# Seven half products for twelve of the 22 up tiles of each SwiGLU block, in a two-layer fp32 transformer on one Trainium2 core

## The reference

```
def rms_norm(x, g):
    y = xf * lax.rsqrt(jnp.mean(xf * xf, axis=-1, keepdims=True) + NORM_EPS)
    return (y * g.astype(jnp.float32)).astype(x.dtype)
def swiglu(h, w1, w3, w2):
    return (jax.nn.silu(h @ w1) * (h @ w3)) @ w2
...
        x = x + 0.5 * rms_norm(swiglu(rms_norm(x, g[0]), ffn_w1[l, 0], ffn_w3[l, 0], ffn_w2[l, 0]), g[1])
...
        x = x + 0.5 * rms_norm(swiglu(rms_norm(x, g[4]), ffn_w1[l, 1], ffn_w3[l, 1], ffn_w2[l, 1]), g[5])
```

## Time and profile before

| what | value |
|---|---|
| three runs | 1973.55, 1974.46, 1974.59 us; median 1974.46 us |
| profiled execution: device time | 1972.13 us |
| its span | 1970.0 us |
| mean granted TensorE clock | 0.993 of full speed |

### The profile page before, as it was taken

One profiled execution on the slowest core, in us unless ns is written; L12 is line 12 of the kernel. 1 busy time (PEld: TensorE's weight loads), 2 busy tenths in 40 slices (PEclk: granted clock), 3 DMA queues, 4 the chain that ended last, 5 costly groups with the idle time before them and its releaser, 6 DMA issues.

```text
span 1970.0 us, 25894 instructions
## 1 busy us (share of the span) xinstructions
PE 1926.0 (98%) x9965; PEld 1652.0 (84%) x9965; DVE 976.3 (50%) x1438; ACT 699.4 (36%) x1099; POOL 48.6 (2%) x55
## 2 busy tenths in 40 slices
PE   8999999999999999999999999999988999999998
PEld 7888888978889888888988888889877898888888
DVE  5444432476757544432385444324766485444323
ACT  5232222355536232322352323223554453232222
POOL 0000000011100000000000000000000000000000
PEclk9999999999999999999999999999999999999999
DMA  5333333322212333333233332333211223333331
GB/s 162 107 98 94 100 93 106 87 65 76 75 54 87 106 90 101 94 101 96 84 86 107 85 106 85 96 104 83 60 42 45 65 78 95 106 87 102 102 94 43
DMA packets 347366, 174.65 MB, mean 89 GB/s; under 512 B 18478, under 2 KB 346268, under 8 KB 347292
## 3 DMA queue, kind: packets, MB, share of 16 engines
q1 hardware_dynamic: 346528, 172.51, 30.8%
q10 hardware_dynamic: 764, 1.11, 0.2%
HBM read 171.50 MB, written 2.10 MB: 88 GB/s over the span
## 4 chain that ended last, share of the span: by engine, by line
PE 89%; DVE 8%; ACT 1%; issue 1%; POOL 0%; DMA 0%; SPq 0%; DVEq 0%; ACTq 0%
PE acc L1425 26%; PE acc L1426 26%; PE acc L1427 26%; PE sco L1425 3%; PE sco L1427 2%; PE sco L1426 2%; DVE sqs L1035 1%; DVE y L982 1%; DVE xT L989 1%; DVE xg L959 1%; DVE wl L924 1%; DVE mx L1123 1%; PE acc L1610 1%; PE aux L1453 1%; PE aux L1425 1%
## 5 line engine op out<-in xcount | busy, mean ns | idle before, releaser
L1425 PE MATMUL acc<-xg,wh 128*128 128x512 f32 (+1 forms) x1816 | 673.1, 371 | 6.5 <-DVE wl L924 2.9
L1426 PE MATMUL acc<-xg,wh 128*128 128x512 f32 (+1 forms) x1816 | 667.3, 367 | 0.0
L1427 PE MATMUL acc<-xg,wl 128*128 128x512 f32 (+1 forms) x1816 | 667.2, 367 | 0.0
L924 DVE TENSOR_TENSOR wl<-raw,wh 128x1024 fp32r<-128x1024 f32 (+1 forms) x332 | 385.6, 1187 | 156.8 <-ACT wh L560 151.7
L1425 PEld LDWEIGHTS acc<-xg,wh 128*128 128x128 f32 x1816 | 343.6, 189 | 64.7 <-DVE wl L924 3.2
L1426 PEld LDWEIGHTS acc<-xg,wh 128*128 128x128 f32 x1816 | 343.5, 189 | 57.0 <-issue 1.4
L1427 PEld LDWEIGHTS acc<-xg,wl 128*128 128x128 f32 x1816 | 343.5, 189 | 55.8
L560 ACT ACTIVATE wh<-raw 128x1024 fp32r<-128x1024 f32 (+1 forms) x332 | 327.1, 1023 | 130.4 <-PE acc L1427 85.9
L1427 PE MATMUL acc<-hT,wl 128*128 128x512 f32 (+1 forms) x704 | 255.2, 362 | 0.0
L1426 PE MATMUL acc<-hT,wh 128*128 128x512 f32 (+1 forms) x704 | 255.2, 362 | 0.0
L1425 PE MATMUL acc<-hT,wh 128*128 128x512 f32 (+1 forms) x704 | 255.2, 362 | 0.0
(11 more groups left out here) (242 smaller groups left out, 1854.6 us busy)
## 6 DMA issues: line engine op xcount, KB each, us to landing
raw<-in_ffn_w_dram SPq DMA_DIRECT2D x240, 512.0 KB, 4.6
raw<-in_ffn_w_dram SPq DMA_DIRECT2D x32, 384.0 KB, 3.4
raw<-in_moba_w_qkv_dram SPq DMA_DIRECT2D x24, 512.0 KB, 3.8
raw<-in_moba_w_o_dram SPq DMA_DIRECT2D x8, 512.0 KB, 3.9
raw<-in_mla_w_o_dram SPq DMA_DIRECT2D x8, 512.0 KB, 4.0
xin<-in_x_dram SPq DMA_DIRECT2D x4, 512.0 KB, 5.6
raw<-in_mla_w_dq_dram SPq DMA_DIRECT2D x4, 512.0 KB, 4.1
raw<-in_mla_w_uq_dram SPq DMA_DIRECT2D x8, 256.0 KB, 2.8
```

Of the source, the lines that this page charges most:

```text
L924: v.tensor_tensor(wl[:, slot, 0:tiles], raw[:, slot, 0:tiles], f32(wh[:, slot, 0:tiles]), ALU.subtract).then_inc(w_lo, 1)
L1425: t.matmul(dst, w_h, m_h, start=start, stop=False)
L1426: t.matmul(dst, w_h, m_l, start=False, stop=False)
L1427: return t.matmul(dst, w_l, m_h, start=False, stop=stop)
```

## The change

Six of the 22 up tiles (`FS`) stay as they were. The other sixteen come in four turns of four (`TURN`): three fast tiles and a plain one.

A fast tile takes w1 and w3 of one inner tile together with the two halves of K (`KH` = 4 of the eight K tiles) and the two token halves as 2x2 blocks, and computes them with seven products in Winograd's form of Strassen's method in place of eight: 7 x 4 x 3 = 84 matmuls of 256 columns, where there were 48 of 512. Four products take sums of weight blocks (`ssum`, and one half of the raw w3 tile rewritten in place) and four take sums of x blocks (`tsum`, split into `tx`, once for each FFN). The products land in `sums`, `pairs` and `rest` (two banks joined), and are added up by one ACT copy (`m1_copied`) and four DVE additions (`second_sum`, `rows`). A fast tile has units of 8, 8 and 12 tiles, which fill three and a half of the four slots, and each fast or plain tile of a turn begins at slot 0; before, units went round the four slots.

So that the products can be added without `Rb`, x is multiplied by gain and norm factor once (`xn`: `x_full` on ACT, two DVE multiplications), and its parts take the place of those of the unnormed x in `xg` (`x_part`) while PE passes from tile 5 to tile 6.

The inner tiles are kept in fp32 (`hid`) through the up half; their high and low parts are made in seven groups (`HID`) where the down half begins. Of a turn's raw tiles each is loaded when the first two weight splits of the tile two before it are done. At the start of the down half ACT makes the high parts of groups 0 and 1, tile 21's silu, the split of the first down unit, groups 2 and 3, the split of the second unit, and then groups and splits in turn. Stages outside the FFNs keep their instructions.

The diff is cut to: the units; ACT's turn (`next_hi` is the weight copy to fp32r); DVE's multiplication by `Rb`, weight sums, product sums, turn (`tile_lo` is the low part of weights) and start of the down half; PE's turn. In the third FFN `x_full` waits for the last key/value unit.

```diff
+    FS, TURN, KH = 6, 4, KD // 2
+    FAST_U = [(UT, 1), (UT, 1), (UT + KH, 0)]
+    TURN_U = FAST_U * (TURN - 1) + [(UT, 1)] * 2
+    TURNS, GT = (KF - FS) // TURN, TURN - 1
+    FFN_U = [(UT, 1)] * (2 * FS) + TURN_U * TURNS + [(n, 1) for n in DOWN] * KD
...
+                        if c < TURN - 1:
+                            g = G0 + GT * it + c
+                            act.wait_ge(prod_psum, 2 * g + 1)
+                            s.activation(usum[:, 0], tile_banks(c)[0][:, half(0)], COPY).then_inc(m1_copied, 1)
+                            next_hi(c, w, 0)
+                            next_hi(c, w, 1)
+                            if c < TURN - 2:
+                                next_hi(c, w, 2)
+                            if q == 0 and c == 1:
+                                x_part(4)
+                            act.wait_ge(rows_ready, 2 * g + 1)
+                            gate(f, T[0][:])
+                        elif not last:
+                            next_hi(c, w, 0)
+                            act.wait_ge(unit_done, w + 1)
+                            gate(f, tile_banks(c)[0][:])
+                            next_hi(c, w, 1)
+                            next_hi(c, w, 2)
...
+                for k in range(0, KD, KH):
+                    dve.wait_ge(xf_ready, KD * nth + k + KH)
+                    v.tensor_tensor(xn[:, k:k + KH], xn[:, k:k + KH],
+                                    Rb[:].unsqueeze(1).broadcast_to([P, KH, S]), ALU.mult).then_inc(xn_ready, 1)
+                plain(2)
+                if kv is not None:
+                    between()
...
+                def outer_sums(w, g, slot, counts):
+                    for a in range(2):
+                        dve.wait_ge(raw_full[slot + a], counts[a])
+                    dve.wait_ge(w_lo, w)
+                    v.tensor_tensor(ssum[:, UT:UT + KH], raw[:, slot, 0:KH], raw[:, slot + 1, 0:KH], ALU.subtract
+                                    ).then_inc(ssum_ready, 1)
+                    dve.wait_ge(ssum_ready, 4 * g + 1)
+                    v.tensor_tensor(raw[:, slot + 1, 0:KH], raw[:, slot + 1, 0:KH], raw[:, slot + 1, KH:KD], ALU.add
+                                    ).then_inc(ssum_ready, 1)
+                def inner_sums(g, slot):
+                    dve.wait_ge(ssum_ready, 4 * g + 2)
+                    v.tensor_tensor(ssum[:, 0:KH], raw[:, slot + 1, 0:KH], raw[:, slot, 0:KH], ALU.subtract
+                                    ).then_inc(ssum_ready, 1)
+                    dve.wait_ge(ssum_ready, 4 * g + 3)
+                    v.tensor_tensor(ssum[:, KH:UT], raw[:, slot, KH:KD], ssum[:, 0:KH], ALU.subtract
+                                    ).then_inc(ssum_ready, 1)
...
+                def second_sum(g, banks):
+                    dve.wait_ge(m1_copied, g + 1)
+                    dve.wait_ge(prod_psum, 2 * g + 2)
+                    v.tensor_tensor(usum[:, 3], banks[0][:, half(1)], usum[:, 0], ALU.add).then_inc(usum_ready, 1)
+                def rows(f, w, g, banks):
+                    rest = banks[2][:, 0:3 * HALF].rearrange("p (a s) -> p a s", a=3)
+                    dve.wait_ge(unit_done, w + 3)
+                    dve.wait_ge(usum_ready, 2 * g + 1)
+                    dve.wait_ge(rows_ready, 2 * g)
+                    v.tensor_tensor(usum[:, 1:3], rest[:, 1:3], usum[:, 3:4].broadcast_to([P, 2, HALF]), ALU.add
+                                    ).then_inc(usum_ready, 1)
+                    dve.wait_ge(usum_ready, 2 * g + 2)
+                    v.tensor_tensor(T[0][:], banks[1][:], usum[:, 0:2].rearrange("p a s -> p (a s)"), ALU.add
+                                    ).then_inc(rows_ready, 1)
+                    dve.wait_ge(hid_ready, F0 + f)
+                    v.tensor_tensor(T[2][:].rearrange("p (a s) -> p a s", a=2), rest[:, 0:2],
+                                    usum[:, 2:3].broadcast_to([P, 2, HALF]), ALU.add).then_inc(rows_ready, 1)
...
+                        if c < TURN - 1:
+                            g = G0 + GT * it + c
+                            if n < TURN - 1:
+                                outer_sums(w_next, g_next, slot, counts)
+                            tile_lo(w_next, 0, slot)
+                            second_sum(g, banks)
+                            if n < TURN - 1:
+                                inner_sums(g_next, slot)
+                            tile_lo(w_next, 1, slot)
+                            rows(f, w, g, banks)
+                            if n < TURN - 1:
+                                tile_lo(w_next, 2, slot)
+                            dve.wait_ge(rows_ready, 2 * g + 2)
+                            gated(f, dst, T[2][:])
+                            if q == 0 and c == 1:
+                                x_part(4)
+                        elif not last:
+                            outer_sums(w_next, g_next, slot, counts)
+                            inner_sums(g_next, slot)
+                            tile_lo(w_next, 0, slot)
+                            dve.wait_ge(unit_done, w + 2)
+                            gated(f, dst, banks[1][:])
+                            tile_lo(w_next, 1, slot)
+                            tile_lo(w_next, 2, slot)
...
+                d0 = down_unit(u)
+                hidden_lo(0)
+                hidden_lo(1)
+                split(d0)
+                dve.wait_ge(unit_done, d0)
+                gated(KF - 1, hid[:, KF - 1], tile_banks(KF - 1)[1][:])
+                hidden_lo(2)
+                hidden_lo(3)
+                split(d0 + 1)
+                hidden_lo(4)
+                split(d0 + 2)
...
+                        pe.wait_ge(hid_ready, KF * nth + f - 1)
+                        pe.wait_ge(w_lo, w + 1)
+                        if c == TURN - 1:
+                            first(xb_lo, 5 * nth + 5)
+                            tiles(sums[:], 0, 0, UT, from_x(xg)).then_inc(unit_done, 1)
+                            pe.wait_ge(w_lo, w + 2)
+                            tiles(pairs[:], 1, 0, UT, from_x(xg)).then_inc(unit_done, 1)
+                            continue
+                        first(xb_lo, 5 * nth + 1)
+                        tiles(sums[:, half(0)], 0, 0, KH, quarter(0, 0)).then_inc(prod_psum, 1)
+                        first(xb_lo, 5 * nth + 3)
+                        tiles(pairs[:, half(0)], 0, KH, KH, quarter(1, 0)).then_inc(unit_done, 1)
+                        pe.wait_ge(w_lo, w + 2)
+                        first(tx_lo, 4 * nth + 2)
+                        tiles(rest[:, HALF:2 * HALF], 1, 0, KH, xsum(0))
+                        tiles(rest[:, 0:HALF], 1, KH, KH, xsum(1)).then_inc(unit_done, 1)
+                        pe.wait_ge(w_lo, w + 3)
+                        first(tx_lo, 4 * nth + 4)
+                        pe.wait_ge(m1_copied, GT * TURNS * nth + GT * it + c + 1)
+                        tiles(sums[:, half(1)], 2, 0, KH, xsum(2)).then_inc(prod_psum, 1)
+                        first(xb_lo, 5 * nth + 4)
+                        tiles(pairs[:, half(1)], 2, KH, KH, quarter(1, 1))
+                        tiles(rest[:, 2 * HALF:3 * HALF], 3, 0, KH, xsum(3)).then_inc(unit_done, 1)
```

More of the change, by code:

```diff
@@ L1535, in ffn @@
                         unit(u + 4 + a, acc[a][:], from_x(xg))
[L1536 to L1541 removed]
+                for i in range(4 * first, 2 * FS - 1):
+                    pe.wait_ge(evacuated, r + i - 3)
+                    unit(u + i, acc[i % 4][:], from_x(xg))
```

386 lines of the change are left out of this document (297 added, 89 removed).

## The result

| | before | after |
|---|---|---|
| median of the runs | 1974.01 us (4 runs, 1973.01 to 1974.59) | 1946.62 us (4 runs, 1943.06 to 1947.78) |
| profiled execution | 1972.13 us, span 1970.0 | 1946.04 us, span 1943.8 |
| ratio | | 0.9859, 95% interval 0.9842 to 0.9876 |

The account below looks back on a forecast made before the run. PE's matmul stream was taken as the bound: 1972.1 - 38.4 (products) + 0.7 (normed x) + 4.0 (down half) + 4.7 (third FFN) + 1.6 (clock) = 1944.7, plus 2.3 for the median: 1947 us; own range 1942 to 1952, 0.8 range 1937 to 1960.

Parts of the forecast that it names:

- PE's pace: Up tiles: a 256-column matmul takes 0.120 us, so a fast tile takes 10.08 us against a plain tile's 10.88.
- The 38.4 us: Products in the up halves: 0.80 us less per fast tile, 48 fast tiles, certain if PE is never kept waiting.
- DVE in a fast tile: DVE's twelve operations take about 9.6 of 10.08 us: nearly saturated, but no PE wait inside the turns.
- With all of DVE's operations 10% longer: Sensitivity in the turns: PE would wait 3.4 us an FFN; at 15% 7.5, at 20% 11.6.
- the rival at 1960: DVE operations 10% slower than the rows say, adding 13.6 us of PE waits; chance 0.18.
- DVE the bound: Rival: DVE 20% slower bounds the fast tiles, 46 us of waits, 1993 us, slower than before; chance 0.05.
- Going over to the normed x: At tile 6 PE's second product waits 0.2 us for the third quarter part, four times: 0.7 us.
- Start of the down half: PE waits 1.0 us for the second unit's low part, behind DVE's groups 2 and 3; four times, 4.0 us.
- The third FFN: Tile 3: PE waits 4.4 us for `ckv_diag` behind DVE's two multiplications of x; 4.7 us with tile 3's first-unit delay.
- the 0.3: Third FFN: `x_full` on ACT delays the split of tile 3's first unit, making PE wait 0.3 us.
- The clock: After the third FFN's 4.4 us pause, one half-clock stretch costs 1.6 us, bounds 0 and 1.6.
- The sum: All terms give 1944.7 us for the profiled execution; 2.3 more for the median of the runs gives 1947.

Follow-up runs that it names:

- the halved loop: Kernel before the change with every matmul of the looped up tiles cut into two of 256 columns: 2023.08 us against 1971.71, ratio 1.0264.
- two extra additions: Changed kernel with two more DVE additions of 512 elements in each fast tile, results unused: 1950.82 us, ratio 0.9886.
- the missing product: Changed kernel with one of a fast tile's seven products (12 of 84 matmuls) left out, output wrong: 1905.02 us, ratio 0.9648.
- the key/value move: Changed kernel with the third FFN's DVE multiplications of x put behind `ckv_diag` and tile 4's weight splits: 1944.23 us, ratio 0.9867.
- both moves: Changed kernel with x's multiplications behind `ckv_diag` in the third FFN, and `hidden_lo(2)` ahead of DVE's wait for the last up product: 1941.02 us, ratio 0.9841.
- turns of eight and of sixteen: Both moves plus 14 fast tiles per FFN in two turns of eight, or 15 in one of sixteen: 1932.81 us (0.9807) and 1931.42 us (0.9794).
- the pause of 2.1: Both moves with 15 fast tiles, and ACT making the first three parts of the normed x ahead of tile 5's silu: 1926.15 us, ratio 0.9765.

## Why the prediction was right, point by point

**PE's pace.** 0.120 a matmul, 10.08 a fast tile, 0.80 to 0.82 less: right, to the hundredth, and confirmed alone by the halved loop. The 38.4 us that were priced came. By the formula of the Trainium skill's page "TensorE: Matmul & The Clock Gate", section "Back-to-back issue gap", the isolated gap for 256 columns is 109.2 ns, and by this estimate the products would have saved 57 us. The trace does not agree: the measured 120 is 10% above it, in the kernel before, the changed kernel and the halved loop alike.

**DVE in a fast tile.** 9.6 us was the sum, 9.45 the measure: right that it is the nearly full engine and that no wait arises inside the turns. Wrong was the sensitivity beside it. "With all of DVE's operations 10% longer" was given 3.4 us an FFN and 15% 7.5; two extra additions lengthen DVE's fast tile by 13%, from 9.45 to 10.65, and cost 0.53. (Two more operations in a queue are not the same as slower ones all along it, which no run has.) Two links of the chain can be read: its fast tile was 0.15 too long, and it left 0.4 us to spare at the third units of the first turn, where the rows have 1.57 and 1.88; in the later turns it had 1.4 and the rows have 1.7 to 1.9. So the rival at 1960 was priced too high for its condition, while "DVE the bound" had its mechanism and place right, as the missing product shows.

**Going over to the normed x.** 0.2 an FFN; the starts give 0.17 on one interval (0.29) and 0.10 on the next (0.22): 0.27.

**Start of the down half.** Mechanism, place and releaser right, 1.0 predicted, 1.18 measured: the pause is 1.04, and the restart's 0.1 was not in the term.

**The third FFN.** 4.7 predicted, 4.05 measured (of -5.23 against -9.29). Tile 3's first unit was not delayed by `x_full`: it starts at 1024.70, 0.81 behind the mean of squares, as in the kernel before, so the 0.3 was nothing, and DVE made the way to the diagonal in 0.2 to 0.3 less. What the prediction did not see is that the wait is a backlog of DVE and not only the order of the two multiplications. Its chain of times does carry `x_full`'s 5.1 us, since DVE's first split ends at 1040.2 there, but as the reason it names only the 4.5 us of the order, and only that was moved. DVE's late start of 4.1 us is about as large, and which part of the 3.8 us it is stays open.

**The clock.** The step that failed as stated: one stretch of 1.6 was put down as sure to follow. In the first profile it did not come. In six profiled executions with this pause at the spread it came in five. It cost 1.6 us in three of them (1.59, 1.64, 1.59) and 2.4 and 2.6 in two, where the spread's own matmuls ran at half clock too, above the bound of 1.6 that was given. With a pause of the same length at tile 6 it came in all four (the key/value move, both moves, turns of eight and of sixteen), and after the pause of 2.1 it did not come.

**The sum.** Without the clock the terms give -29.0, the trace -28.4. The profiled execution then stands 2.2 higher in code that did not change: 1.1 before tile 2 of the first FFN (42.46 against 41.36), where eleven more matmuls of 256 columns start 0.21 apart in place of 0.12, and 1.0 in the attention of layer 1, with six half-clock stretches against five (below). The forecast was 1944.7 for the profiled execution, which took 1946.04, and added 2.3 for the median, which lies only 0.6 above it. That the median falls within 0.4 us of the forecast is partly chance: a missing 1.6 and an unforeseen 2.2 in the trace, and an allowance 1.7 too large on top of it.

## What to carry to other kernels

Fewer columns in smaller matmuls are worth what the fixed part of each matmul leaves: price both forms from starts in the trace first (here 0.2267 and 0.120, so an eighth fewer columns are 7% of the tile). When another engine fills up, compare its work with the bound engine's per tile, and add up what it overdraws over the full tiles that follow each other; set that against the spare time at the first place where the bound engine wants its result. Here 2 x 0.57 us too much per turn used up nearly all of the spare time (0.06 to 0.19 us were left at the third unit of the third fast tile) and cost 0.13 a turn. In the kernel without the third product it was 2 x 0.81, with the spare time shorter by the product's 1.44 as well, and it cost 1.7 a turn, though DVE was idle for 6.2 us of the same turn. A wait that moves when the order is changed is a backlog: look for what stands idle on the other engines meanwhile (here ACT's parts behind a silu) and for what the late engine itself waited for before the backlog began (here `x_full`), not only for another place of the same work.
